# Row tables of the expert groups as bf16 parts in a mixture-of-experts kernel on one core

## What is computed

```python
def moe(h, w_router, b_router, w_gate_e, w_up_e, w_down_e, w_gate_s, w_up_s, w_down_s):
    t = h.reshape(bsz * l, d)                                   # 384 tokens x 1024
    scores = jax.nn.sigmoid((t @ w_router).astype(jnp.float32)) # 64 experts
    _, idx = lax.top_k(scores + b_router.astype(jnp.float32), TOP_K)   # 8 of them
    sel = jnp.take_along_axis(scores, idx, axis=-1)
    wts = sel / jnp.sum(sel, axis=-1, keepdims=True) * ROUTED_SCALE
    combine = jnp.sum(jax.nn.one_hot(idx, N_EXPERTS, dtype=jnp.float32) * wts[..., None], axis=1)
    hg = jnp.einsum('td,edf->tef', t, w_gate_e)                 # per expert 1024 x 256
    hu = jnp.einsum('td,edf->tef', t, w_up_e)
    act = jax.nn.silu(hg) * hu * combine[..., None].astype(t.dtype)
    routed = jnp.einsum('tef,efd->td', act, w_down_e)
    shared = (jax.nn.silu(t @ w_gate_s) * (t @ w_up_s)) @ w_down_s
    return (routed + shared).reshape(bsz, l, d)
```

## Time and profile before

| | us |
|---|---|
| median of 3 runs | 955.38 (955.33 to 955.88) |
| profiled execution | 957.51 |
| its span, first to last instruction | 955.8 |
| PE busy | 910.9 (95%) |
| DVE busy | 426.2 (45%) |
| ACT busy | 187.8 (20%) |
| POOL busy | 94.7 (10%) |

### The profile page before, as it was taken

The page is one execution under the profiler, slowest core; times in us unless marked ns, Lnnn a source line. Parts: engine busy times, 40 slices in busy tenths (PEclk is TensorE's granted clock), DMA queues, the critical chain, the costliest instruction groups (busy, mean ns, idle before and its releaser), DMA issues.

```text
span 955.8 us, 13246 instructions
## 1 busy us (share of the span) xinstructions
PE 910.9 (95%) x4997; PEld 487.7 (51%) x4997; DVE 426.2 (45%) x770; ACT 187.8 (20%) x309; POOL 94.7 (10%) x198
## 2 busy tenths in 40 slices
PE   5999999999999999999999999989999989899995
PEld 2455567676555687544444444434445453454432
DVE  4129966534762346463333333323233323323267
ACT  3150601212100013112212212111111211211111
POOL 2000000000000000202112111111111201111100
PEclk9999999999999999999999999999999999999998
DMA  9998453625677356799999999999999999999995
GB/s 344 355 404 327 132 201 142 229 89 177 237 292 269 125 245 240 279 395 374 420 419 420 420 420 420 420 421 421 419 421 419 421 423 418 423 420 420 420 418 220
DMA packets 85034, 322.04 MB, mean 337 GB/s; under 512 B 10084, under 2 KB 38936, under 8 KB 56040
## 3 DMA queue, kind: packets, MB, share of 16 engines
q1 hardware_dynamic: 70368, 289.43, 76.3%
q0 software_dynamic: 9216, 22.22, 6.0%
q10 hardware_dynamic: 5384, 9.51, 2.8%
HBM read 298.36 MB, written 34.11 MB: 348 GB/s over the span
## 4 chain that ended last, share of the span: by engine, by line
PE 88%; DMA 5%; DVE 2%; issue 2%; ACT 2%; SPq 1%; DVEq 0%; POOLq 0%
PE bank L624 25%; PE bank L1910 22%; PE bank L653 13%; PE bank L2096 4%; PE bank L2082 4%; PE bank L610 3%; DMA arena<-expert_rows 3%; PE bank L2002 2%; PE bank L2124 2%; PE bank L604 2%; PE bank L577 2%; PE bank L1886 1%; PE bank L642 1%; PE bank L2194 1%; ACT arena L635 1%
## 5 line engine op out<-in xcount | busy, mean ns | idle before, releaser
L624 PE MATMUL bank<-arena 128*32 128x512 f32 (+2 forms) x1568 | 256.8, 598 | 9.0 <-issue 9.0
L1910 PE MATMUL bank<-arena 128*128 128x384 f32 x640 | 211.6, 490 | 2.4 <-ACT arena L1697 2.4
L624 PEld LDWEIGHTS bank<-arena 128*32 128x32 f32 (+2 forms) x1568 | 89.8, 123 | 171.7 <-issue 171.6
L1910 PEld LDWEIGHTS bank<-arena 128*128 128x128 f32 x640 | 121.1, 191 | 86.5 <-issue 7.0
L653 PE MATMUL bank<-arena 128*32 128x512 f32 (+2 forms) x784 | 131.5, 596 | 4.9 <-issue 4.2
L653 PEld LDWEIGHTS bank<-arena 128*32 128x32 f32 (+2 forms) x784 | 43.1, 122 | 69.8 <-issue 69.1
L658 DVE SCALAR_TENSOR_TENSOR arena<-bank,arena 128x512 f32<-128x512 f32 x36 | 27.0, 751 | 106.5 <-PE bank L653 106.3
L666 ACT ACTIVATE arena<-arena 128x1024 f32<-128x1024 f32 x36 | 41.3, 1148 | 163.1 <-DVE arena L662 159.3
L463 DVE SCALAR_TENSOR_TENSOR arena<-arena 128x2048 f32<-128x2048 f32 x28 | 64.6, 2348 | 18.8 <-DMA arena<-in_w_mod_dram 17.7
L638 DVE TENSOR_TENSOR arena<-arena,bank 128x256 f32<-128x256 f32 x36 | 21.9, 607 | 85.6 <-ACT arena L635 85.6
L570 DVE TENSOR_TENSOR arena<-arena 128x288 f32<-128x288 f32 (+3 forms) x64 | 22.0, 380 | 82.1 <-POOL arena L741 41.1
(11 more groups left out here) (262 smaller groups left out, 794.7 us busy)
## 6 DMA issues: line engine op xcount, KB each, us to landing
arena<-in_w_up_e_dram SPq DMA_DIRECT2D x64, 1024.0 KB, 29.2
arena<-in_w_down_e_dram SPq DMA_DIRECT2D x64, 1024.0 KB, 29.2
arena<-in_w_gate_e_dram SPq DMA_DIRECT2D x64, 1024.0 KB, 27.0
arena<-in_w_mod_dram SPq DMA_DIRECT2D x24, 1024.0 KB, 7.5
arena<-in_w_in_dram SPq DMA_DIRECT2D x22, 1024.0 KB, 7.7
expert_rows<-arena SPq DMA_DIRECT2D x6, 2048.0 KB, 22.4
arena<-expert_rows SPq DMA_DIRECT2D x12, 1024.0 KB, 24.9
arena<-in_w_out_dram SPq DMA_DIRECT2D x4, 1024.0 KB, 5.4
```

The costliest lines, as they stand in the source:

```text
L624: ins = pe.matmul(bank[off:off + width, :], x_T[:, k, off:off + width], w[:, :, k, :], start=(k == 0), stop=(k == KT - 1))
L1910: ins = pe.matmul(ps[:, 0:TOK], w[:, k, P * (n % 2):P * (n % 2) + P], hT[:, k, :], start=(k == 0), stop=(k == KT - 1))
```

## The change

The row table is made of bf16 values in place of fp32. The four fp32 values of a token become eight bf16 ones: the first three, which do not depend on the expert (two fixed parts and the partition's number), stay in `qv` from the start, written once (12 fills); the choice number's low part and the weight as three bf16 parts are copied by `pick` from `traits`; the eighth is zero. Each of the first numbers is a sum of two parts that bf16 holds exactly. The places stand apart in fp32 (`qplace`), so `pick` makes two copies in place of one. `table` gets one more product that adds the offset `FAR` to every row; `row_numbers` adds the parts up, in five instructions for four. `values` splits the weights into three parts. For the groups in `ON_CHIP` the table is written a second time in fp32 (`gather_hot`). Two semaphores are merged into `consts`.

```diff
-        vals = at(a_rows, NT, NE, 4)
-        onehot = [at(a, NT, ROWS) for a in (a_rows + 768, a_rows + 768 + NT * ROWS)]
+        place_of = at(a_rows, NT, NE)
+        traits = at(a_rows + NT * NE, 2 * NT * NE).bitcast(BF16).rearrange("p (t e v) -> p t e v", t=NT, v=4)
+        a_hot = a_rows + 3 * NT * NE
+        gather_hot = at(a_hot, NT, ROWS)
...
         def pick(pool, b, s, e):
-            return pool.tensor_copy(qv[:, b % 2, s], vals[:, :, bass.ds(e, 1), :].rearrange("p t e v -> p t (e v)"))
+            pool.tensor_copy(qv[:, b % 2, s, :, 3:7], traits[:, :, bass.ds(e, 1), :].rearrange("p t e v -> p t (e v)"))
+            return pool.tensor_copy(qplace[:, b % 2, s, :], place_of[:, :, bass.ds(e, 1)].rearrange("p t e -> p (t e)"))
...
         def table(pe, b, s, off, width):
             for o, w in [(32, 32), (64, 64)] if (off, width) == (32, 96) else [(off, width)]:
+                pe.matmul(banks[7][o:o + w, 0:8], ones_half[:, o:o + w], far, start=True, stop=False)
                 for t in range(NT):
-                    ins = pe.matmul(banks[7][o:o + w, 0:4], onehot[b][:, t, o:o + w], qv[:, b % 2, s, t, :],
-                                    start=(t == 0), stop=(t == NT - 1))
+                    ins = pe.matmul(banks[7][o:o + w, 0:8], onehot[b][:, t, o:o + w], qv[:, b % 2, s, t, :],
+                                    start=False, stop=(t == NT - 1))
...
-        def row_numbers(dve, b):
-            dve.tensor_tensor(rows_i[:, b, :], banks[7][:, 1:3], far, ALU.add)
-            dve.tensor_scalar(of_seq[:, 0, b:b + 1], banks[7][:, 1:2], CTX - FAR, None, ALU.is_lt)
-            dve.tensor_scalar(of_seq[:, 1, b:b + 1], banks[7][:, 1:2], CTX - FAR, None, ALU.is_ge)
-            return dve.tensor_copy(wt[:, b:b + 1], banks[7][:, 3:4])
+        def row_numbers(dve, x, b, times):
+            dve.tensor_reduce(row_sums, banks[7][:, 0:4].rearrange("p (j v) -> p v j", v=2), AX.X, ALU.add)                .then_inc(x["summed"], 1)
+            dve.tensor_scalar(of_seq[:, 0, b:b + 1], banks[7][:, 0:1], float(CTX), None, ALU.is_lt)
+            dve.tensor_scalar(of_seq[:, 1, b:b + 1], banks[7][:, 0:1], float(CTX), None, ALU.is_ge)
+            dve.tensor_reduce(wt[:, b:b + 1], banks[7][:, 4:7], AX.X, ALU.add)
+            dve.wait_ge(x["summed"], times)
+            return dve.tensor_copy(rows_i[:, b, :], row_sums)
...
                 for s, (rank, off, width) in enumerate(QUADS[i]):
-                    ins = mark(dve, i % 2, s, off, width)
+                    ins = mark(dve, onehot[i % 2], i, s, off, width)
+                    if i in ON_CHIP:
+                        ins = mark(dve, gather_hot, i, s, off, width)
...
-                dve.tensor_scalar(vals[:, t, :, 1], ones[:, 0:NE], tok_far[:, 0, one], None, ALU.mult)
-                dve.tensor_scalar(vals[:, t, :, 2], rank[:, t, :], tok_far[:, 1, one], None, ALU.add)
-                link(dve.tensor_scalar(vals[:, t, :, 3], scores[:, t, :], weight_sum[:, one], ROUTED_SCALE,
+                dve.tensor_scalar(traits[:, t, :, 0], rank[:, t, :], low, None, ALU.add)
+                link(dve.tensor_scalar(scores[:, t, :], scores[:, t, :], weight_sum[:, one], ROUTED_SCALE,
                                        ALU.mult, ALU.mult))
+                for part in (1, 2):
+                    link(dve.tensor_copy(traits[:, t, :, part], scores[:, t, :]))
+                    link(dve.tensor_tensor(scores[:, t, :], scores[:, t, :], traits[:, t, :, part], ALU.subtract))
+                link(dve.tensor_copy(traits[:, t, :, 3], scores[:, t, :]))
...
+            for b in range(2):
+                for s in range(2):
+                    dve.tensor_copy(qv[:, b, s, :, 0:2], static.rearrange("p v t -> p t v"))
+                    dve.tensor_copy(qv[:, b, s, :, 2:3], part_f.unsqueeze(1).to_broadcast([P, NT, 1]))
+                    link(dve.memset(qv[:, b, s, :, 7:8], 0.0))
```

More of the change, by code:

```diff
@@ L56 @@
 NXS = 6
-FAR = 8192.0
+FAR = 4096.0
 FIXED = 3
@@ L357, in program @@
         part_f = at(take(1), 1)
-        far = at(take(2), 2)
+        far = at(take(4), 4).bitcast(BF16)
+        row_sums = at(take(2), 2)
+        low = at(take(1), 1)
+        low_i = at(take(1), 1).bitcast(I32)
         most_f = at(take(1), 1)
         most_i = at(take(1), 1).bitcast(I32)
-        tok_far = at(take(2 * NT), 2, NT)
+        static = at(take(2 * NT), 2, NT)
         of_seq = at(take(8), 2, 4)
@@ L476, in piece_arrived @@
             eng.wait_ge(done, 16 * among * times)
-        ex_names = ("picked onehot_done tab_done rows_ready rows_seen xtr_done xT_a xT_b gu_done sil_done act_done "
+        ex_names = ("summed picked onehot_done tab_done rows_ready rows_seen xtr_done xT_a xT_b gu_done sil_done act_done "
                     "actp_done actT_done y_done y_a y_b gate_begun gate_done").split()
@@ L605, in rows_to_features, with rows_from_tokens @@
             return ins
-        def rows_from_tokens(pe, b, part):
+        def rows_from_tokens(pe, part):
             for k in part:
@@ L610, in rows_from_tokens @@
                     ins = pe.matmul(banks[k // 4][:, P * (k % 4):P * (k % 4) + P], h2[:, t, P * k:P * k + P],
-                                    onehot[b][:, t, :], start=(t == 0), stop=(t == NT - 1))
+                                    gather_hot[:, t, :], start=(t == 0), stop=(t == NT - 1))
             return ins
@@ L739, in prepare @@
                         link(ins)
-                        place = qv[:, i % 2, s, :, 0:1]
+                        place = qplace[:, i % 2, s, :]
                         ins = pool.tensor_scalar(place, place, -1.0, float(width + 1), ALU.mult, ALU.add)
@@ L803, in transpose_x @@
                     pe.wait_ge(x["onehot_done"], i + 1)
-                    ins = rows_from_tokens(pe, i % 2, range(4 * part, 4 * part + 4))
+                    ins = rows_from_tokens(pe, range(4 * part, 4 * part + 4))
                 else:
@@ L892, in one_hot @@
                     dve.wait_ge(x["tab_done"], i - 1)
-                if i - 2 in ON_CHIP:
-                    dve.wait_ge(x["xtr_done"], i - 1)
+                before_it = [j for j in ON_CHIP if j < i]
+                if i in ON_CHIP and before_it:
+                    dve.wait_ge(x["xtr_done"], before_it[-1] + 1)
                 for s, (rank, off, width) in enumerate(QUADS[i]):
-                    ins = mark(dve, i % 2, s, off, width)
+                    ins = mark(dve, onehot[i % 2], i, s, off, width)
+                    if i in ON_CHIP:
+                        ins = mark(dve, gather_hot, i, s, off, width)
                 ins.then_inc(x["onehot_done"], 1)
@@ L904, in numbers @@
                     n = i - ADDED
-                    dve.tensor_scalar(token_of[:, n:n + 1], banks[7][:, 1:2], FAR, None, ALU.add)
-                row_numbers(dve, i % 4).then_inc(x["rows_ready"], 1)
+                    dve.tensor_reduce(token_of[:, n:n + 1], banks[7][:, 0:4].rearrange("p (j v) -> p v j", v=2)[:, 0, :],
+                                      AX.X, ALU.add)
+                row_numbers(dve, x, i % 4, i + 1).then_inc(x["rows_ready"], 1)
             def x_half(i):
@@ L1061, in dve_spill @@
                 dve.wait_ge(x["picked"], n + 1)
-                mark(dve, 2, 0, 0, ROWS).then_inc(x["onehot_done"], 1)
+                mark(dve, onehot[2], 2, 0, 0, ROWS).then_inc(x["onehot_done"], 1)
                 dve.wait_ge(x["tab_done"], n + 1)
-                row_numbers(dve, NQ % 4).then_inc(x["rows_ready"], 1)
+                row_numbers(dve, x, NQ % 4, n + 1).then_inc(x["rows_ready"], 1)
                 dve.wait_ge(x["xtr_done"], n + 1)
@@ L1435, in vector_part_b @@
             full(dve, job)
-            free(dve.scalar_tensor_tensor(out=vals[:, :, :, 0],
+            free(dve.scalar_tensor_tensor(out=place_of,
                                           in0=bank(job)[:, 0:NT * NE].rearrange("p (t e) -> p t e", t=NT), scalar=1.0,
@@ L1562, in _ @@
                 if u == ("k", 0):
-                    sp.wait_ge(S["no_rows_ready"], 1)
+                    sp.wait_ge(S["consts"], 3)
                     for t in range(NT):
@@ L1974, in _ @@
             drained(pe, ("lrp",))
-            pe.wait_ge(S["strips_ready"], 1)
+            pe.wait_ge(S["consts"], 2)
             job = ("lr",)
```

42 lines of the change are left out of this document (26 added, 16 removed).

## The result

| | before | after |
|---|---|---|
| median, measured together, us | 956.13 (955.33 to 956.97) | 958.8 (956.52 to 959.49) |
| ratio | | 1.0022, 95% interval [1.0012, 1.0032] |
| the same kernel again beside the experiments | | 1.0016 [1.0007, 1.0025] and 1.0012 [1.0003, 1.0020] |
| profiled execution (its span) | 957.51 (955.8) | 956.52 (954.8) |

The change costs about 1.5 us, 0.15%: some 1.1 us of it can be followed in the traces. (The first ratio is close to that of the means, 958.36 and 956.17; the two medians alone would give 1.0028, as the seven runs of after lie apart, two near 956.7 and five near 959.) The profiled execution of after is the fastest of its seven, and shorter than that of before, so the spans can't be compared: their difference has to be taken apart first.

The account below looks back on a forecast made before the run. Full DMA engines from 440 us were taken to bound the kernel, the end moving with the last load release before: 1.95 - 0.35 = +1.6 us on the median 955.38 gives 957.0 us, range 955.0 to 958.7.

Parts of the forecast that it names:

- slower: Outcome for the whole kernel: its time rises by over 0.2%; chance 0.39.
- What bounds: DMA engines full from 440 to 900 us; the last event releasing loads before that sets the end, PE does not.
- E: Issue of the two `w_down` loads released by group 0's `down` product, about 429 us; forecast to come 1.6 us later.
- (a): DVE, `values(1)`: three closing instructions become seven, +1.2 us; a hidden wait leaves the counts 0.57 later.
- (b): DVE, `values(2)`: +1.2 us again, on the path before POOL's first pick, which comes 1.77 later in all.
- (c): POOL: two copies per expert in place of one, 0.33 us more a group; `one_hot(1)` comes 2.43 later.
- (d): DVE, `row_numbers(0)`: five instructions in place of four, +0.2 us; row numbers of group 0 come 2.6 later.
- (e): PE, `look_up(1)`: starts 1.95 us later, saves 0.3; the shared products behind it and their loads come 1.65 later.
- (f): Gather of group 0's rows moves with the row numbers; PE's transposes begin 1.55 to 2.6 us later, taken as 1.95.
- The rival in which the gather decides: Group 0's gather takes 8.4 us again, PE idles before the transposes, time 958.2 us; chance 0.24.
- (g): PE, `look_up(2)`: 12 records in 0.88 us become 8 in about 0.5, 0.35 us saved.
- Two records per bf16 product: On PE, bf16 products also make two records each, a look-up costs 0.3 to 0.45 us more, about 958.4; chance 0.03.

Follow-up runs that it names:

- early_big: The kernel before with two spare products of 512 columns on PE ahead of the look-up of group 1; ratio to before 1.0018.
- later: The kernel before with the look-ups of groups 6 to 13 made twice; ratio to before 0.9995.
- nosplit: The changed kernel without the splitting of the weights, one broadcast cast per token tile in place of three casts and two subtractions; ratio to before 1.0003.
- places_apart: The changed kernel reordered: POOL copies places of groups 0 and 1 before the traits, takes group 1's numbers after group 0's traits; ratio to before 1.0005.
- best_two: The changed kernel reordered: places early, DVE's shared product ahead of `values(2)`, first look-up later, group 1's numbers in POOL's wait for `values(2)`; ratio to before 1.0008.
- early_places: The changed kernel with POOL copying the places of groups 0 and 1 ahead of `vals_ready`, the traits after it; ratio to before 1.0012.

## Why the prediction was right, step by step

The forecast was +1.6 us, within 0.2% and near the upper edge. The ratios 1.0022, 1.0016 and 1.0012 are 2.1, 1.5 and 1.1 us. The median measured first with it, 958.8, is 0.1 above the upper end of the range: the kernel before measured 0.75 higher there (956.13) than in the runs shown, and the ratio was the highest of the three. That ratio alone would have been "slower" by a hair, the case that had 0.39.

- **What bounds**: right. D follows E, the added work ahead of E costs what it takes (early_big), the work behind it nothing (later), and 11.2 us saved on PE went into waits, near the 33 × 0.35 of the sum.
- **(a), (b), the split**: right. The casts and subtractions follow each other at 0.27; the counts come +0.54 (385.05 against 385.37, plus 0.86; forecast 0.57), POOL's first pick +1.64 (1.77). nosplit gives 1.64 of the first look-up's +1.89 back.
- **(c), POOL**: right in kind, a little smaller: the copies follow each other at 0.13, so a group costs 0.26 more. one_hot(1) comes +2.17 (2.43).
- **(d), row numbers**: +2.25 at their end (2.6), the five instructions at 0.07 each as before, the last without a wait.
- **(e), the second look-up**: +1.65 (1.95). It takes 0.58 in place of 1.00, and the shared products behind it and their loads come +1.23 (1.65).
- **(f), the gather**: this is the step that failed, though it did not decide. I let its landing move with its issue. It was issued +2.25 later, took 7.1 us in place of 8.4 and landed at 403.65, +0.95; the transposes came at 404.07, bound by PE, +1.23 instead of +1.95, and so ahead of the stretch that was given as a sign (404.93 after adding 0.86, not 405.2 to 406.3). The reading under it was wrong as well: in before the transposes were not waiting for the gather. They begin 7.83 behind the shared products (395.87, the first row below, to 403.70, with no idle time), as they do in after (396.24 to 404.07); the gather had landed just ahead of them, by 0.13. The last section shows what the landing goes by. The rival in which the gather decides had the right second limit and the wrong direction: the landing follows its issue so little that it does not delay the changed kernel, but holds back a kernel whose PE would come earlier. PE waited for it by 0.68 in nosplit, 0.53 in places_apart and 0.14 in best_two, and none of them came below before.
- **(g), the third look-up**: 8 records in 0.42 (423.71 to 424.13) against 0.81, 0.39 saved (0.35); only 0.17 reached E, since PE's transposes of the activations (L659), 0.49 behind the look-up's end in before, now come 0.69 behind it. That they wait for a bank which DVE frees is read from the program and was not tried. The rows of before, for (f) and (g):

```profile
395.87 7.99 PE L2124 MATMUL bank<-arena 128*128 128x512 f32 x18
...
424.14 0.66 PE L604 MATMUL bank<-arena 128*128 128x128 f32 x4
424.63 0.38 PE L642 MATMUL bank<-arena 128*128 128x128 f32 x2
```

So 1.95 − 0.35 = 1.6 became 1.23 − 0.17 = 1.06: two terms were too large by 0.5 together, with the right signs. The times say 1.5 (median of 29 runs of after 957.94, of the 71 of before measured beside them 956.49); the 0.4 between lies within the intervals of two of the three ratios, neither the front nor the tail of the profiles shows it, and whether there is anything behind it stays open. That the times lie closer to 1.6 than E does is luck, not a merit of the sum.

"Two records per bf16 product", the rival with 0.03, is refuted by the rows: 8 products are 8 records. As to the four passes of fp32 (the Trainium skill, "FP8 and Floating Point Precision", section "TensorE Precision Notes"): 0.81 us over 6 fp32 products is 0.135 each, 0.42 over 8 bf16 ones 0.053, a factor of 2.6 at this size, less than the four passes of the page alone would give. But the prediction was too quick to say that the trace does not agree: two records are not two passes. In the row of 396.24 the records of the wide shared products, 512 columns each and again two a product, start some 0.43 us apart, which is two cycles of 2.4 GHz for a column, so four for a product. The trace holds no wide bf16 product to set beside it.

## What to carry over

Where the DMA engines are full to the end, ask which event releases the last loads ahead of that stage, and cost a change by how it moves this event alone; what it saves behind it is worth nothing, however often it is saved. Look for the floor under that event as well (here a transfer that lands when the loads ahead of it do): work taken off the path pays only down to the floor, work added pays from it. And count from a mark just ahead of the changed work: two profiles of one kernel can differ by more, at the front and at the tail, than the change is worth.

## What the runs showed of the hardware

**A small gather behind large loads lands with them, at issues that lie 2.3 us apart.** The last 1 MB load ahead of it and the gather in after: the first row is that load's issue, the second its us to landing, and the third the gather's.

```profile
391.55 0.59 SPq L525 DMA_DIRECT2D arena<-in_w_gate_e_dram  x1
```
```profile
DMA to landing us min/median/max: 11.9/11.9/11.9
```
```profile
DMA to landing us min/median/max: 7.1/7.1/7.1
```

The load lands at 403.47, the gather (issued at 396.56) at 403.65. In nosplit, issued 1.65 earlier counted from F, it takes 8.2 us and lands 0.18 behind the load; in before and in best_two it lands 0.64 and 0.63 ahead of it. Over the fourteen profiles the issues lie 28.2 to 30.6 us behind F, the landings 36.4 to 37.7, from 0.79 ahead of that load to 0.31 behind it; with one and the same issue, 28.3, the landing varies by 1.1. In each of them the first packet of the gather moves 4.3 to 4.5 us behind its issue (taken from the DMA packets); from there to the landing it takes 4.0 us in before, beside the loads for longer, and 2.7 in after.

**The granted clock falls in some executions of a kernel and not in others, behind the same work.** It fell behind the wait of 2.43 us at the front in nine profiles of fourteen, behind 2.70 us of products of 4 columns in one of two, behind a wait of 1.47 us in the profile of early_places, and behind waits of 1.41 and 1.42 us in none of three. Among the shared products, where PE is on the path, a fall cost some 1.7 us. What decides it was not found. That the number of slow products varies from run to run is also what the Trainium skill says ("TensorE: Matmul & The Clock Gate", section "What's actually happening"), there of the start of a kernel.
